# Twenty places for expert matrices in one decoder step, with smaller row buffers and fewer unread products

## The reference

```python
pg = softmax(h @ wg); g_sel = argmax(pg)                 # one of 4 groups
pf = softmax((h @ we) of the group g_sel)                # 8 experts in it
top_p, top_i = top_k(pf, 2)
combine[expert of top_i] = max(pg) * top_p / sum(top_p)  # 0 for all other experts
act = silu(h @ w_gate[e]) * (h @ w_up[e]) * combine[e]   # 32 experts, 1024 -> 256
out = sum over e of act @ w_down[e]                      # 256 -> 1024
y = rms_norm(x + gate2 * out)
```

## Time and profile before

| | us |
|---|---|
| median of 3 runs (lowest, highest) | 1347.26 (1346.13, 1348.58) |
| the profiled execution | 1346.08 |
| its span, first to last instruction | 1344.4 |
| TensorE busy | 1274.1 (95%) |
| VectorE busy | 712.5 (53%) |
| gate/up products, L3081, 512 instructions | 116.8 |
| down products, L3104, 256 instructions | 62.0 |
| mean granted TensorE clock | 0.986 |

### The profile page before, as it was taken

One profiled execution on the slowest core, in us unless ns is written; L12 is line 12 of the kernel. 1 busy time (PEld: TensorE's weight loads), 2 busy tenths in 40 slices (PEclk: granted clock), 3 DMA queues, 4 the chain that ended last, 5 costly groups with the idle time before them and its releaser, 6 DMA issues. The chain is left out here.

```text
span 1344.4 us, 19593 instructions
## 1 busy us (share of the span) xinstructions
PE 1274.1 (95%) x6916; PEld 901.9 (67%) x6916; DVE 712.5 (53%) x1441; ACT 264.1 (20%) x580; POOL 290.9 (22%) x411
## 2 busy tenths in 40 slices
PE   7999999999999999998999999989999999998776
PEld 3787667788787787776777777778877743333224
DVE  1734588898887777510012555676567633221126
ACT  3201211222222333330121222310001310000002
POOL 0213334333333334222121111200001121111000
PEclk9999999999999999998999999999999999999999
DMA  9552243323313313655467330531229499999985
GB/s 376 187 114 88 77 136 148 118 71 126 126 63 126 126 63 125 212 192 166 145 204 292 117 124 32 188 130 63 94 71 413 187 353 419 419 419 419 419 362 205
DMA packets 71220, 259.30 MB, mean 193 GB/s; under 512 B 10950, under 2 KB 24550, under 8 KB 57147
## 3 DMA queue, kind: packets, MB, share of 16 engines
q1 hardware_dynamic: 54370, 221.99, 43.6%
q0 software_dynamic: 10112, 20.16, 4.4%
q10 hardware_dynamic: 6648, 15.96, 4.2%
HBM read 238.67 MB, written 27.44 MB: 198 GB/s over the span
## 5 line engine op out<-in xcount | busy, mean ns | idle before, releaser
L371 PE MATMUL psum<-arena 128*128 128x272 f32 x2408 | 568.7, 394 | 6.2 <-DVE arena L1393 1.9
L371 PEld LDWEIGHTS psum<-arena 128*128 128x128 f32 x2408 | 453.5, 190 | 117.4 <-issue 19.4
L393 POOL TENSOR_TENSOR arena<-arena 128x512 f32<-128x512 f32 x96 | 127.5, 1328 | 199.5 <-DMA arena<-in_weights 160.8
L3081 PE MATMUL psum<-arena 128*64 128x512 f32 x512 | 116.8, 604 | 16.0 <-DMA arena<-in_w_gu 13.6
L1537 PE MATMUL psum<-arena 128*128 128x272 f32 x512 | 123.7, 400 | 0.8 <-DVE arena L1702 0.8
L1537 PEld LDWEIGHTS psum<-arena 128*128 128x128 f32 x512 | 96.8, 192 | 26.5 <-DVE arena L1702 4.4
L2007 PE MATMUL psum<-arena 128*128 128x272 f32 x384 | 96.0, 404 | 3.1 <-PEq L213 3.1
L3081 PEld LDWEIGHTS psum<-arena 128*64 128x64 f32 x512 | 36.3, 138 | 85.8 <-issue 69.9
L2007 PEld LDWEIGHTS psum<-arena 128*128 128x128 f32 x384 | 73.1, 195 | 20.4 <-issue 5.6
L1702 DVE TENSOR_TENSOR arena<-arena,psum 128x272 f32<-128x272 f32 x16 | 7.0, 439 | 126.3 <-ACT arena L1633 126.3
L3176 DVE TENSOR_TENSOR arena<-arena,psum 128x256 f32<-128x256 f32 x16 | 6.8, 422 | 122.7 <-ACT arena L3167 122.7
(11 more groups left out here) (403 smaller groups left out, 1444.6 us busy)
## 6 DMA issues: line engine op xcount, KB each, us to landing
arena<-in_weights SPq DMA_DIRECT2D x153, 512.0 KB, 5.1
arena<-in_w_gu SPq DMA_DIRECT2D x64, 1024.0 KB, 23.0
arena<-in_w_down SPq DMA_DIRECT2D x32, 1024.0 KB, 24.8
arena<-in_weights ACTq DMA_DIRECT2D x16, 512.0 KB, 4.3
arena<-in_pages_k POOLq DMA_DIRECT2D x40, 128.0 KB, 4.0
arena<-in_x SPq DMA_DIRECT2D x2, 2176.0 KB, 12.3
y_rows<-arena SPq DMA_DIRECT2D x8, 544.0 KB, 16.8
arena<-in_pages_v SPq DMA_DIRECT2D x32, 128.0 KB, 3.7
```

The costliest lines, as they stand in the source:

```text
L371: mm = pe.matmul(out, lhsT=w[:, c * P:c * P + P], rhs=x[:, c, :], start=(c == 0 and not added), stop=(c == 3), skip_group_check=added or more)
L393: link(dve.tensor_tensor(sums[:, k], a, b, op))
L3081: mm = pe.matmul(psum[CAP * e:CAP * e + CAP, 2 + k, :].rearrange("p (o f) -> p o f", o=2), lhsT=xgT[:, k, lo:lo + CAP], rhs=wv[:, e, c2], ...
```

## The change

- Two more places for matrices (SLOTS = 20): one in the area of the token rows (rows11) just below the place of matrix 14, and one in the router's scratch at a_r11.
- They are made free by smaller buffers: gathered rows xg 4 to 2 (XG = 2, the late pair with its memset gone), turned rows xgT 2 to 1, staged outputs yst 2 to 1. All scatters count on one semaphore, and y_out of pair p waits for all scatters up to that of p-1; last_y_out waits for that of pair 14. In GpSimd's loop the scatter lags by LAG = 3 in place of 4, so gather p stands behind scatter p-4.
- Loads: 15 waits for nothing of its own; 16 (and with it 17) waits until all five row tiles are turned; 18 until the three writes of h2_rows have landed; 19 until the weights are picked. The wait for the first gather is gone. The number of rounds is read ahead of 19.
- keep_busy takes widths: three of 256 columns among the row turns instead of four of 512; behind the ranks 512 once instead of twice; behind the first slots 512 twice instead of three times; behind the second once instead of three times; and a new one of 256 behind the first turn of gathered rows.
- The tail's row buffer yr moves from the ring's area to a_q, whose places hold earlier matrices with the new count.

```diff
-            XG = 4
-            gath = (s_gath, s_gath1, sem("rows_gathered2"), sem("rows_gathered3"))
-            scat = (s_scat, s_scat1)
-            s_rows2 = sem("rows_cleared2")
+            XG, LAG = 2, 3
+            gath = (s_gath, s_gath1)
...
-                a_w - 192 - 2 * W_BLK, a_w - 192 - W_BLK, a_h, a_h + W_BLK)]
+                a_w - 192 - 2 * W_BLK, a_w - 192 - W_BLK, a_h, a_h + W_BLK,
+                a_w - 224 - 3 * W_BLK, a_w + 4 * W_BLK)]
...
-            xgT = A.at(a_e + 2048, 2, DC * P)
-            yst = A.at(a_e + 4096, 2, D)
+            xg_all = A.at(a_e, XG, D)
+            xg = [xg_all[:, i, :] for i in range(XG)]
+            xgT = A.at(a_e + 2048, DC * P)
+            yst = A.at(a_e + 3072, D)
...
-            def keep_busy(pe, bank, n):
+            def keep_busy(pe, bank, *widths):
-                for _ in range(n):
-                    pe.matmul(psum[:, bank, :], lhsT=const("ident"), rhs=xT[:, 0, 0:512], start=True, stop=True)
+                for n in widths:
+                    pe.matmul(psum[:, bank, 0:n], lhsT=const("ident"), rhs=xT[:, 0, 0:n], start=True, stop=True)
...
-                    if i < 4:
-                        keep_busy(pe, 3, 1)
+                    if i < 3:
+                        keep_busy(pe, 3, 256)
...
-                keep_busy(pe, 6, 2)
+                keep_busy(pe, 6, 512)
...
-                        if at == 15:
-                            sp.wait_ge(s_h2w[2], 16)
                         if at == 16:
-                            sp.wait_ge(s_slot, 1)
+                            sp.wait_ge(s_row_ps, NR)
+                        if at == 18:
+                            for k in range(3):
+                                sp.wait_ge(s_h2w[k], 16)
+                        if at == 19:
+                            sp.wait_ge(s_pickw, 1)
                             sp.reg_load(trips, all_counted)
-                            sp.wait_ge(gath[0], 16)
                         block_in(r, at)
...
-                        if p == 2:
-                            pool.wait_ge(s_pickw, 1)
-                            pool.memset(xg_late, 0.0).then_inc(s_rows2, 1)
-                            pool.wait_ge(s_rows2, r + 1)
...
-                        if p >= XG:
-                            k = p % 2
-                            pool.wait_ge(s_yo, r * NP + (p - XG + 2))
+                        if p >= LAG:
+                            pool.wait_ge(s_yo, r * NP + (p - LAG + 2))
...
                 slots(1, 0, True)
-                keep_busy(pe, 6, 3)
+                keep_busy(pe, 6, 512, 512)
                 slots(1, 1, True)
-                keep_busy(pe, 6, 3)
+                keep_busy(pe, 6, 512)
                 with pe.Fori(0, rounds(pe)) as r:
                     turn_x(r, 0)
+                    keep_busy(pe, 6, 256)
...
                     dve.wait_ge(s_dn, r * (2 * NP) + (2 * p + 2 + LEAD))
-                    if k:
-                        dve.wait_ge(scat[1], r * (8 * NP) + (p // 2 + 1) * 16)
-                    elif p:
-                        dve.wait_ge(scat[0], r * (8 * NP) + p // 2 * 16)
+                    dve.wait_ge(s_scat, r * (16 * NP) + (p + 1) * 16)
...
-                    dve.wait_ge(scat[1], r * (8 * NP) + 8 * NP)
+                    dve.wait_ge(s_scat, r * (16 * NP) + 16 * NP)
...
-            yr = A.at(a_ring, NR, 2 * D)
+            yr = A.at(a_q, NR, 2 * D)
```

More of the change, by code:

```diff
@@ L2612, in build @@
             a_e = a_q + 8192
-            xgT = A.at(a_e + 2048, 2, DC * P)
-            yst = A.at(a_e + 4096, 2, D)
-            actb = A.at(a_e + 6144, 2, FF)
-            actT = A.at(a_e + 6656, 2, 2 * P)
-            sil = A.at(a_e + 7168, 2, FF)
+            xg_all = A.at(a_e, XG, D)
+            xg = [xg_all[:, i, :] for i in range(XG)]
+            xgT = A.at(a_e + 2048, DC * P)
+            yst = A.at(a_e + 3072, D)
+            actb = A.at(a_e + 4096, 2, FF)
+            actT = A.at(a_e + 4608, 2, 2 * P)
+            sil = A.at(a_e + 5120, 2, FF)
             tab_i = A.at(a_e + 7680, NP).bitcast(I32)
             gat_i = A.at(a_e + 7680 + NP, NP).bitcast(I32)
-            assert a_e + 7680 + 2 * NP <= a_w - 192 - 2 * W_BLK
+            assert a_e + 7680 + 2 * NP == a_w - 192 - 2 * W_BLK and a_e + 5632 == a_w - 224 - 3 * W_BLK
             (s_sq11, s_ss11, s_std11, s_xs, s_xs7, s_xn, s_acc, s_hs11, s_rt, s_rl, s_ge, s_gi, s_pe2,
@@ L2658, in build @@
             tmp32 = A.at(a_r + 1200, 2, NR * NE)
-            assert a_r11 + (XG - 2) * D <= a_r + 1520
+            assert a_r11 == a_w + 4 * W_BLK and a_r11 + W_BLK <= a_r + 1520
             rank = A.at(a_r + 1520, 2 * NR)
@@ L2944, in _ @@
                                    ALU.subtract).then_inc(p_link11, 1)
-                pool.memset(xg_early, 0.0).then_inc(s_rows, 1)
+                pool.memset(xg_all, 0.0).then_inc(s_rows, 1)
                 pool.wait_ge(s_rnew, 1)
@@ L2959, in last_pair @@
                     pe.matmul(psum[:, 4 * half + c // 2, c % 2 * 256:c % 2 * 256 + 256],
-                              lhsT=yst[:, 1, c * P:c * P + P], rhs=slot_tok[:, 256 * half:256 * half + 256],
+                              lhsT=yst[:, c * P:c * P + P], rhs=slot_tok[:, 256 * half:256 * half + 256],
                               start=(c % 2 == 0), stop=False, skip_group_check=True)
@@ L3017, in _ @@
                     pool.wait_ge(s_rows, 1)
-                    for p in range(NP + XG - 1):
+                    for p in range(NP + LAG - 1):
                         k = p % XG
-                        if p == XG:
+                        if p == LAG:
                             pool.wait_ge(s_yo, r * NP + 1)
@@ L3024, in _ @@
                                 out=y_rows, out_offset=bass.IndirectOffsetOnAxis(tab_last, 0),
-                                in_=yst[:, 1, :], in_offset=None,
-                                bounds_check=last_row, oob_is_err=False).then_inc(scat[1], 16)
-                        if p == 2:
-                            pool.wait_ge(s_pickw, 1)
-                            pool.memset(xg_late, 0.0).then_inc(s_rows2, 1)
-                            pool.wait_ge(s_rows2, r + 1)
+                                in_=yst, in_offset=None,
+                                bounds_check=last_row, oob_is_err=False).then_inc(s_scat, 16)
                         if p < NP:
@@ L3040, in _ @@
                                 bounds_check=last_token, oob_is_err=False).then_inc(gath[k], 16)
-                        if p >= XG:
-                            k = p % 2
-                            pool.wait_ge(s_yo, r * NP + (p - XG + 2))
+                        if p >= LAG:
+                            pool.wait_ge(s_yo, r * NP + (p - LAG + 2))
                             pool.sem_inc(s_passed, 1)
                             pool.indirect_dma_start(
[L3046 to L3050, removed]
+                                out=y_rows, out_offset=bass.IndirectOffsetOnAxis(tab_i[:, p - LAG:p - LAG + 1], 0),
+                                in_=yst, in_offset=None,
+                                bounds_check=last_row, oob_is_err=False).then_inc(s_scat, 16)
+                    pool.wait_ge(s_scat, r * (16 * NP) + 16 * NP)
                     pool.sem_inc(s_round, 1)
@@ L3081, in gate_up @@
                                 mm = pe.matmul(psum[CAP * e:CAP * e + CAP, 2 + k, :].rearrange("p (o f) -> p o f", o=2),
[L3082 removed]
+                                               lhsT=xgT[:, lo:lo + CAP], rhs=wv[:, e, c2],
                                                start=(c == 0), stop=(c == DC - 1))
@@ L3207, in x_out @@
                     dve.wait_ge(s_xps, r * NP + (p + XG + 1))
-                    dve.tensor_tensor(xgT[:, p % 2, :].rearrange("p (c n) -> p c n", n=P),
+                    dve.tensor_tensor(xgT.rearrange("p (c n) -> p c n", n=P),
                                       psum[:, 0:2, :].rearrange("p a (c n) -> p (a c) n", n=P),
@@ L3360, in last_pair_new @@
                     for c in range(DC):
-                        pe.matmul(turned(c, 4), lhsT=yst[:, 1, c * P:c * P + P], rhs=slot_tok[:, SEQ:NT],
+                        pe.matmul(turned(c, 4), lhsT=yst[:, c * P:c * P + P], rhs=slot_tok[:, SEQ:NT],
                                   start=(c == 0), stop=False, skip_group_check=True)
```

8 lines of the change are left out of this document (2 added, 6 removed).

## The result

The changed kernel is slower by 0.49%: ratio to the kernel before 1.0049, 95% interval 1.0037 to 1.0061, which is +6.6 us on 1347.1. Its five runs have a median of 1354.81 us (1350.6 to 1355.93), those of before beside them 1347.12. The profiled executions lie further apart, 1355.93 us and 1346.08, spans 1354.3 and 1344.4. Of these 9.9 us, 3.9 are lost ahead of the change. The first matrix was issued at 1013.54 against 1009.65, and the granted clock tells why. In the windows of before (stretch, us, busy of PE, PEld, DVE, ACT, POOL, clock, DMA share, GB/s)

The account below looks back on a forecast made before the run. The expert stage was taken as bound by matrix transfers through full DMA engines. Four early matrices -4.5 us, TensorE's shift +2.7 and tail +3.2 gave +1.4 us: 1348.7 us, range 1343.0 to 1354.0.

Parts of the forecast that it names:

- The case taken as the likeliest: Whole kernel: a difference under 0.2% (2.7 us), not to be told from no change; chance 0.43.
- the rival of the late first gather: Start of expert stage: writes last, gather 7.8 us, low clock 1.7, sum +6.2 us, 1353.5 us; chance 0.27.
- d: Expert stage start: shift of TensorE's start, 1.8 us from the first gather plus 0.9 from the clock, +2.7 us.
- What bounds the stage: Expert stage: transfer of 96 matrices of 1 MiB at 418 GB/s, 2.5 us each, DMA full from 1090 to 1300.
- Four matrices are worth 10 us, less d: Expert stage: queue full from matrix 20 with 76 to come, not 16 with 80; four at 2.50 us sent ahead.
- The row writes land at 1080.7: Before the first gather: row writes sharing engines alike with matrices 16 and 17 land at 1080.7, the middle value.
- writes last: Before the first gather: late end of the range, row writes finishing behind matrices 16 and 17, at 1082.9.
- The gather takes 6.0 us: First gather, issued at 1082.1 behind 18 and 19: lands after 6.0 us, at 1088.1, against 4.2 us before.
- Low clock 0.9 us: TensorE's first turn and products after 6.5 us idle: half clock costs 0.9 us, between 0 and 1.7.
- Smaller unread products, 1.8 us sooner and nothing at the end: Row turns and ranks: rank product 1.8 us sooner; by itself buys nothing, since the first turn waits for the gather.
- Gathers one pair later, one transposed tile, the memset: Expert stage: gather p follows scatter p-4, single turned tile, second memset of 1.8 us gone; no cost or gain.
- The tail +3.2: After the last matrix: y_out 14 waits for scatter 13 (+5.3 us), y_rows loads go later, tail +3.2 us.

Follow-up runs that it names:

- e2: Changed kernel with matrix 15 again waiting for the row writes and 16 for the first gather's landing: ratio 1.0016 to the kernel before, +2.2 us.
- e5: Changed kernel with the earlier waits of matrices 15 and 16, and pair 14's output staged in a free gather buffer with its own semaphore: ratio 1.0001 to the kernel before.
- e7: Kernel before with only the changed kernel's smaller and fewer unread products (keep_busy edits): ratio 0.999 to the kernel before, -1.3 us.
- e6: Changed kernel, pair 14's output staged in a free gather buffer; 16 and 17 wait for the third row write, 18 and 19 for the first gather: ratio 0.998, -2.7 us.
- e8: Changed kernel, pair 14's output staged in a free gather buffer; 16 to 19 wait for the row writes only, not the first gather: ratio 0.9992, -1.1 us.
- e10: Changed kernel, free gather buffer for pair 14's output, 16 to 19 after the row writes, six more unread 512-column products before the first turn: ratio 0.9998.
- e4: Changed kernel with ten more unread products of 512 columns ahead of the first turn of gathered rows: ratio 1.0046 to the kernel before, +6.2 us.
- e3: Changed kernel with pair 14's output staged in a free gather buffer, its scatter on its own semaphore: ratio 1.0018 to the kernel before, +2.4 us.
- e1: Kernel before, two buffers kept, with y_out and last_y_out waiting for all scatters up to the pair before: ratio 1.0023 to the kernel before, +3.1 us.

## Why the prediction was partly wrong

The two places were the right ones, and the range was wide enough for the ratio (1347.26 x 1.0049 = 1353.9) but not quite for the median of the five runs (1354.81 against 1354.0). The case taken as the likeliest, no change that can be told, was not the one that came; the rival of the late first gather was, at +6.2 against +6.6 measured. The forecast's direction was right; its size, +1.4 us, was too small because of d, the shift of TensorE's start.

- **What bounds the stage**: right. DMA at 1.01 and 418 GB/s from 1108 on, TensorE idle at times.
- **Four matrices are worth 10 us, less d**: right; 9.7 by the table. With d = 8.6 the formula gives +4.1 and the profile shows +2.5, as the changed kernel's row of the table is the lowest of its kind (219.2).
- **The row writes land at 1080.7** (71.0 us): this step failed first. I took equal service in bytes; they landed at 74.2 us, later than my bound of "writes last" (1082.9, 73.3 us). The queues had equal service in packets, and a matrix's packets are twice as large (211 of 1.60 MB against 213 of 0.82 MB): matrices 16 and 17 together, twice the bytes of the second write, have as many packets as it, so it ends with them, not ahead of them. And the bound had forgotten that 15 delays the first write too: it took 6.0 us instead of 4.0. This step alone put the first gather 3.2 us later than forecast, more than half of the 5.9 us by which d was missed.
- **The gather takes 6.0 us**: 7.3; the row of 7.8 was the nearer one. In the later profiles it took 4.4 to 5.4 us with the old waits (e2, e5, e7) and 8.1 to 9.5 with 16 and 17, or all four, issued just ahead of it (e6, e8 to e10). That is 1.3 us more of d.
- **Low clock 0.9 us**: 2.0 in the changed kernel's profile against e4, but 0.9 in e3, which starts alike. The size was right for most executions and 1.1 us short for this one. All three terms erred to one side here: d was taken as 2.7 and was 8.6.
- **Smaller unread products, 1.8 us sooner and nothing at the end**: the rank product came 1.8 us sooner (profile), but it was not for nothing: where 16 waits for the gather, it moves the transfers' end, by 2.1 us in e2's profile and 0.7 in e7's; no ratio tells such an amount.
- **Gathers one pair later, one transposed tile, the memset**: nothing that shows: e5, which has them, and e7, which has not, end their transfers at 305.6 us both, with tails of 28.4.
- **The tail +3.2**: +3.4 in the profile; its cause is shown by e1 (there alone) and e3 (taken away). y_out 14 started 5.3 us later against y_out 13 than before, as worked out. That the size fits is in part luck. The loads were to go 5.3 us later against the last matrix and went 3.7 later, as scatter 14 landed in 5.5 us instead of 7.6; the five loads took 14.0 us, not 12.9; and the 0.7 us of low clock were not in the sum. In e1, e2 and e4 the same wait cost 4.3 to 4.8.

The rule of the Trainium skill that each DMA engine serves its queues in turn ("DMA: Bandwidth & Descriptors", Queues, rings and completion order) agrees with the trace: 211 packets of one queue went beside 213 of the other. The prediction made a half share of the bytes of it, which gave 71.0 us where 74.2 was measured; a turn each by packets gives the matrices two thirds, as their packets are twice as large. The clock's fall after an idle array ("TensorE: Matmul & The Clock Gate", Part 1) agrees: the granted clock was 0.50 from 1.1 us into the 9.11 idle us until 5.6 us after them, and 1.00 throughout with the array kept busy in e4.

What stays open: how much the writes would gain from larger packets of their own or smaller ones of the matrices. No run here varied the size or the queue of the transfers; the turn by packets is read from the traces alone. A single profile of each kernel does not separate a gather of 8.1 from one of 9.5 us.

## What to carry to other kernels

In a stage bound by transfers, reckon from the moment at which the queue becomes full for good: each transfer ahead of it is worth its own time (about 2.4 us here), and each us by which the first release comes later costs one. A bulk load issued beside a short transfer that everything waits for made that short one 1.7 to 3.4 times as long here. Look at the packets as well as the bytes: two queues that take turns by packets share the bytes as their packet sizes do. Holding the bulk loads until the short one has landed won the loss back (e2, e5); sending some of them in between, as in e6, gained 2.7 us with an interval that begins at 0.3. A buffer made single turns the landing of its last reader into a wait: look for the two closest uses, not the usual distance, and for the engine that falls idle behind that wait, whose lower clock is then part of the price.

## What the runs showed that I had not expected

- Two busy DMA queues shared the engines by packets, not by bytes: 211 packets with 1.60 MB of matrices beside 213 with 0.82 MB of row writes in 6 us.
- A write of 128 KiB, issued 1.5 us behind one of 1 MiB on the same queue and with two loads of 1 MiB on another, took 9.8 us to land (2.9 with no loads beside it).
- A gather of 128 rows took 4.2 to 5.4 us beside little, 7.3 to 9.5 with two to four matrices issued just ahead.
- Executions of the same kernel on one chip spread by 12 us (before: 1342.77 to 1355.01 in 35 runs), with stretches of low clock at places that change from one execution to the next; 12 runs of a kernel still left intervals of 0.12% to 0.2% to each side.
